# Issuing the V gather ahead of the U gather in every tick of a single-core encoder step

## The reference, cut to what matters

```python
s1 = jnp.einsum('thd,nd->thn', qh[:, :, 0], keys1)      # 8 heads, scores against 128 keys
s2 = jnp.einsum('thd,nd->thn', qh[:, :, 1], keys2)
...
e = i1[ci // 16] * 128 + i2[ci % 16]                     # 16 experts of 16384 for each token and head
gate = softmax(sc)
act = gelu(einsum('td,thkd->thk', xb, u_tab[e])) * gate  # a dot with a row of U for each expert
out = einsum('thk,thkd->td', act, v_tab[e])              # a weighted sum of the same experts' rows of V
```

## Time and profile before

| | |
|---|---|
| timed runs, device us | 3309.31, 3309.66, 3315.91 (median 3309.66) |
| the profiled execution, device us | 3304.53 |
| its span, first to last instruction | 3302.3 us |
| TensorE, VectorE, GpSimd busy | 79%, 69%, 61% of the span |
| indirect DMAs | 2112, 1107.43 MB in all |

### The profile page before, as it was taken

The page is one execution under the profiler, slowest core; times in us unless marked ns, Lnnn a source line. Parts: engine busy times, 40 slices in busy tenths (PEclk is TensorE's granted clock), DMA queues, the critical chain, the costliest instruction groups (busy, mean ns, idle before and its releaser), DMA issues.

```text
span 3302.3 us, 42154 instructions
## 1 busy us (share of the span) xinstructions
PE 2607.0 (79%) x11764; PEld 1183.6 (36%) x11764; DVE 2282.9 (69%) x6088; ACT 648.6 (20%) x2367; POOL 2004.0 (61%) x2131
## 2 busy tenths in 40 slices
PE   7687888778887788778887788778887788777666
PEld 2563453234422453234422453234422453233111
DVE  2454987678756887679756887578766887679453
ACT  2221222111211222111211122112211222111111
POOL 0132567665776567665766567665776567665775
PEclk9798999878997889878987899878997889888557
DMA  7354999999999999999999999999999999999998
GB/s 263 135 197 166 387 363 394 416 390 344 396 405 403 377 368 395 409 391 349 399 402 398 376 368 398 407 392 343 404 413 400 371 368 399 403 398 359 398 399 362
DMA packets 340171, 1213.81 MB, mean 368 GB/s; under 512 B 41072, under 2 KB 41200, under 8 KB 339904
## 3 DMA queue, kind: packets, MB, share of 16 engines
q0 software_dynamic: 304128, 1107.43, 85.8%
q1 hardware_dynamic: 35776, 103.32, 8.3%
HBM read 1205.73 MB, written 4.87 MB: 367 GB/s over the span
## 4 chain that ended last, share of the span: by engine, by line
PE 25%; DMA 25%; DVE 24%; issue 15%; POOL 6%; ACT 3%; POOLq 0%; DVEq 0%; ACTq 0%; SPq 0%
DMA ring<-peer_v,idxv 16%; PE bank L458 15%; PE acc L458 10%; DMA ring<-peer_u,idx 9%; DVE ring L1434 8%; POOL ring L434 6%; DVE kw L1211 2%; DVE eh L1222 1%; DVE kw L1221 1%; DVE topi L1213 1%; DVE kw L1219 1%; ACT xn L857 1%; DVE idxv L1269 1%; DVE tops L1212 1%; DVE topi L1214 1%
## 5 line engine op out<-in xcount | busy, mean ns | idle before, releaser
L458 PE MATMUL acc<-ring,wv 128*32 128x512 f32 x4224 | 1312.9, 709 | 540.4 <-DMA ring<-peer_v,idxv 417.7
L1434 DVE SCALAR_TENSOR_TENSOR ring<-ring,xcur 128x1024 f32<-128x1024 f32 x1056 | 1283.6, 1218 | 656.4 <-DMA ring<-peer_u,idx 630.6
L434 POOL DMA_INDIRECT ring<-peer_u,idx x1056 | 1006.6, 953 | 817.7 <-issue 416.3
L434 POOL DMA_INDIRECT ring<-peer_v,idxv x1024 | 964.0, 941 | 433.5 <-issue 277.1
L458 PEld LDWEIGHTS acc<-ring,wv 128*32 128x32 f32 x4224 | 171.3, 115 | 1203.2 <-issue 662.7
L458 PEld LDWEIGHTS bank<-xT,win 128*128 128x128 f32 (+1 forms) x2304 | 276.2, 190 | 108.5 <-issue 92.9
L458 PE MATMUL bank<-xT,win 128*128 128x128 f32 (+1 forms) x2304 | 307.1, 290 | 6.8 <-DVE kw L1232 4.3
L857 ACT ACTIVATE wv<-rep,coefv 128x32 f32<-128x32 f32 x1024 | 264.3, 312 | 109.4 <-PE acc L458 79.4
L458 PEld LDWEIGHTS bank<-xT,qk 128*128 128x128 f32 x1024 | 160.1, 246 | 64.5 <-issue 64.5
L458 PE MATMUL bank<-win,xT 128*128 128x512 f32 (+3 forms) x368 | 177.3, 614 | 1.9 <-ACT xT L857 1.9
L458 PE MATMUL bank<-xT,qk 128*128 128x128 f32 x1024 | 173.1, 338 | 0.0
(11 more groups left out here) (232 smaller groups left out, 2213.8 us busy)
## 6 DMA issues: line engine op xcount, KB each, us to landing
qk<-wq SPq DMA_DIRECT2D x64, 512.0 KB
t<-wq SPq DMA_DIRECT2D x64, 512.0 KB, 6.9
ring<-peer_u,idx POOLq DMA_INDIRECT x1056, 6.5
ring<-peer_v,idxv POOLq DMA_INDIRECT x1024, 6.6
win<-w_in SPq DMA_DIRECT2D x6, 2048.0 KB, 15.3
ring<-wq SPq DMA_DIRECT2D x16, 512.0 KB, 5.2
wout<-w_out SPq DMA_DIRECT2D x1, 4096.0 KB, 22.4
xn<-x_prompt SPq DMA_DIRECT2D x8, 512.0 KB, 6.9
```

What stands on the lines that cost most here:

```text
L434: pool.indirect_dma_start(out=ring[:, slot, :], out_offset=None, in_=(peer_u, peer_v)[which], in_offset=bass.IndirectOffsetOnAxis(ap=rows_ ...
L458: return nc.tensor.matmul(out, lhsT, rhs, start=start, stop=stop)
L1434: stt(row, row, 1.0, xcur[:, :], ALU.mult, ALU.mult, accum_out=dots[:, column(b, e):column(b, e) + 1]).then_inc(s_dot, 1)
```

## The change

The order of the two gathers in a tick is turned round, V first and then U, in the plain ticks (`side_by_side`) and in those that carry one block's last V rows over into the next (`over`). The first 18 gathers (U rows of the sample tokens) and the last 18 (V rows of the last block) keep their places. `row_of` moves the places in the ring to match: U rows after the first 18 of the sample tokens go to odd places, V rows to even ones. The users' programs on VectorE, TensorE and ScalarE keep their order, and no count of gathers, bytes or waits changes.

```diff
             lead = 2 * SAMPLE + LAG
             if b is None:
-                turns, place = 0, 2 * e + LAG + 1 if which else e if e < LAG else 2 * e - LAG
+                turns, place = 0, 2 * e + LAG if which else e if e < LAG else 2 * e - LAG + 1
             elif which:
-                turns, place = b * (2 * P // RING), lead + 2 * e + 1
+                turns, place = b * (2 * P // RING), lead + 2 * e
                 if is_count(b, BLOCKS - 1) and e >= P - LAG:
                     place = lead + e + P - LAG
             elif e >= LAG:
-                turns, place = b * (2 * P // RING), lead + 2 * e - 2 * LAG
+                turns, place = b * (2 * P // RING), lead + 2 * e - 2 * LAG + 1
             else:
-                turns, place = (b - 1) * (2 * P // RING), lead + 2 * (P - LAG) + 2 * e
+                turns, place = (b - 1) * (2 * P // RING), lead + 2 * (P - LAG) + 2 * e + 1
             return place % RING, (turns + place // RING + 1) * 16
...
             def side_by_side(b, ticks):
-                return [x for t in ticks for x in ((U, b, t), (V, b, t - LAG))]
+                return [x for t in ticks for x in ((V, b, t - LAG), (U, b, t))]
 
             def over(b):
 
                 last = (None, SAMPLE - LAG) if is_count(b, 0) else (b - 1, P - LAG)
-                return [x for t in range(LAG) for x in ((U, b, t), (V, last[0], last[1] + t))]
+                return [x for t in range(LAG) for x in ((V, last[0], last[1] + t), (U, b, t))]
```

## The result

| | median of timed runs | ratio to the kernel before, 95% interval |
|---|---|---|
| before | 3309.31 us (3300.65 to 3315.91, 5 runs) | |
| after | 3340.30 us (3329.13 to 3349.58, 5 runs) | 1.0101 [1.0069, 1.0133] |

The prediction said 3307 us with a range of 3294 to 3322. The change costs 31 us by the medians. The profiled execution of the changed kernel took 3349.58 us (span 3347.3, mean granted TensorE clock 0.842; before 3302.3 and 0.852), so the two traces lie 45 us apart and show more loss than the medians do.

What follows compares the result with a forecast made beforehand. VectorE was taken to bound each block's search stretch, DMA the rest. Hand-overs -4.2, DMA stretch +4.3, start -2.5, tail 0 gave -2.4 us: 3304.53 to 3302.1 profiled, 3307 in timed runs, range 3294 to 3322.

Steps and rivals of the forecast that it cites:

- What bounds the kernel: Each block has a search stretch, where VectorE sets the end (108.33 of 120 us busy), then a DMA-bound stretch.
- The DMA stretch: Rest of each block after about tick 41: stalled V gathers hold U rows, 0.6 us a block, 4.3 us lost.
- The hand-over: Ticks 1 to 7 of each block: VectorE's wait for scores goes, U(6) comes later; 0.6 us a block, 4.2 won.
- The start: Before block 0: V(14) no longer issued behind U(0), VectorE's 3.13 us wait goes; 2.5 us won, bounds 0 and 3.1.
- The tail: Last 18 V gathers: the last U row comes one issue (1.24 us) later; costs nothing, at most 1.2 us.
- Rival B: U row behind a stalled V row, in hand-overs and DMA stretch: slower, up to 3324 us, middle 3317; chance 0.27.

Runs made afterwards that it cites:

- both ties gone: V first everywhere, weight matrices made two experts ahead and tick 49's spread in PSUM bank 3; 3313.21 us, ratio 1.0001 to the kernel before.
- U first with the same edits: Kernel before with weight matrices made two experts ahead and tick 49's spread in PSUM bank 3; 3295.17 us, ratio 0.9966 to the kernel before.
- v_first_0_41: V first only in ticks 0 to 41 of each block and in the sample tokens; 3314.29 us, ratio 1.0022 to the kernel before.
- u_first_42_58: V first in every tick but 42 to 58, where U is first; 3337.63 us, ratio 1.0089 to the kernel before.

## Why the prediction was wrong, point by point

**What bounds the kernel.** Right, and it held after the change (VectorE's free time in the middle stretch of the earlier trace rows is 27%, not 26%).

**The DMA stretch** (+4.3 us, bounds 0 and 17.4). This step failed. It said "If TensorE's sums come earlier by the same 2.5 us there, nothing changes", and priced the other case at no more than two issues (2.5 us) in a block. Measured from dot 40 to 64 alone: +39.7 us in the profiled execution. The sums did not come earlier by the same amount, since `wv` and tick 49 are tied to VectorE, whose pace had not changed. A V row that lands a tick sooner and waits for something else then holds its slot up to a tick longer: from issue to the end of its sum 8.3 us before and 9.7 after on average in ticks 40 to 47, 8.5 and 9.9 in ticks 48 to 55. When GpSimd waits for nothing else, a slot comes up again after 8 issues of 1.24 us, 9.9 us, and a longer hold stops the stream: of the 64 V rows issued in ticks 48 to 55, 4 were held longer than that before and 29 after. The upper bound was wrong because a stall was counted as one issue (1.24 us), while V(36) alone waited up to 5.19 us, and because the slower projection behind some of TensorE's waits was not in it. The rows needed were in the trace of before: what `expert_sum` waits for besides the row (259.7 and 115.3 us for `wv`) was not looked up. The cause is shown for the 21.9 us of dots 52 to 56. The 12.1 us of dots 40 to 46 are close to what the term had meant, one issue more for a U row in each block (8 x 1.24 = 9.9 us), but no run shows that this is their cause.

**The hand-over** (-4.2 us, bounds 0 and -12.6). The mechanism was right in part: V(116) earlier, U(6) behind it, the wait at L1210 gone or below 1 us in all seven blocks, dot 6 waiting for `peer_u`. The sign was wrong: +3.4 us in seven hand-overs, and +0.19% with the order changed there alone. Only U(6) was followed. Dots 4 and 5 were already waiting for their rows before, and dot 5 now starts 2 us later, so that the time won at the scores was gone before dot 6. U(6) itself took longer than the 6.5 us assumed: issued at 1452.28, its dot began when it had landed, at 1460.35, 8.1 us later. The fit in the Trainium skill, "DMA: Bandwidth & Descriptors", section "Anatomy of one DMA — SWDGE (gpsimd) path", gave an estimate of 4.4 us; the measurement decides.

**The start** (-2.5 us). Its mechanism is seen: TensorE's wait for V(14) is 1.66 us instead of 5.28, the wait of 3.13 us for the scores is gone, dot 6 waits 1.04 us. That dot begins 3.0 us sooner (328.12 against 331.08), but 1.8 us of it were there when U(0) was issued (304.33 against 306.10; over all runs of all kernels that time lies between 304.3 and 309.3), so some 1.2 us are its own.

**The tail** was put at nothing, at most 1.2 us. From the last dot to the end the traces have 32.7 us before and 33.9 after, which a single pair can't tell from none: over all kernels it lies between 30.6 and 34.7.

**Rival B**, the U row behind a stalled V row, was right in sign and in the signs it named: waits for `PE acc` and for `peer_u` rose. It was priced at 3324 at most because it took the stalls at one issue each, and placed half of them at the hand-over.

**What stays open.** With both ties gone V first is still 0.35%, some 12 us, behind U first with the same edits. The traces name two candidates. One is the entry again: dots 40 to 46 take 11.4 us longer there (134.6 against 123.2), and V first from tick 42 on has this loss in every kernel, by 7 to 13 us in six pairs with the same edit, while `v_first_0_41` and `u_first_42_58` don't have it (118.4 and 117.5 against 119.0 before). The other is the hand-over: 310.8 against 302.4 us in seven of them. The traces of that pair lie 34.8 us apart, much more than the medians, so they don't say how the 12 us are shared. No run tells the two apart together with the edits. Single profiled executions differ from the medians by up to 13 us, so the idle times above place the stalls but don't add up to the medians.

## What to carry to other kernels

Before a transfer is moved forward, list everything that its user waits for. If another operand or a shared bank comes at an unchanged time, an earlier landing only holds the slot longer, and with a shared in-order queue it holds the other stream too. A queue runs free as long as every slot is given back within one turn of the ring; compare that with the measured hold before changing an order. The turn is as long as the pace makes it. Here it is 9.9 us when nothing else holds the queue; in the search stretch, where VectorE's dots set the pace, four ticks take 14 us (dots 8 to 40: 899.9 us in eight blocks), and there the hold rose from 10.4 to 12.3 us in ticks 20 to 39 at a cost of only 2.4 us in all. If one tie is removed and its stall goes but the time stays, look for the next tie and remove both before judging.

## What the runs showed of the hardware

A short wait on TensorE can cost more than its length. Behind waits of 1.27, 2.12, 2.50 and 2.33 us the next projection of 16 matmuls took 3.66, 3.56, 3.76 and 3.65 us, about 1.6 us more than the usual 2.03 to 2.05. The granted clock says why: 0.53 over the 3.66 us at 1227.61 of the changed kernel, against 1.00 over the 2.03 us at 1214.66 before, so most of it ran at the 1.2 instead of the 2.4 GHz level. It does not follow every such wait: behind the 1.47 us for V(31) in the kernel with both edits the projection took 2.03. Counted over the changed kernel's trace, for each of its 240 projections with the longest idle time directly ahead of it or of the two groups of matmuls before it: of 57 with 1.2 to 2.6 us 30 took over 3 us, of 102 with at most 0.4 us none did. The last of the four cases is from the hand-over:

```profile
1458.80 1.05 PE L458 MATMUL acc<-ring,wv 128*32 128x512 f32 x4 [2.33 <-DMA ring<-peer_v,idxv]
1459.78 3.65 PE L458 MATMUL bank<-xT,qk 128*128 128x128 f32 x16
```
